# A ring of six row buffers in place of eight under the expert gathers of a hybrid decoder layer

## What is computed

```python
e = i1 * PEER_KEYS + i2
gate = jax.nn.softmax(c_top, axis=-1)
act = jax.nn.gelu(jnp.einsum('thkd,td->thk', u_tab[e], xt).astype(jnp.float32), approximate=False)
w = (gate * act).astype(xt.dtype)
return jnp.einsum('thk,thkd->td', w, v_tab[e])
```

## Time and profile before

| What | us |
|---|---|
| Median of 3 runs (lowest, highest) | 3116.35 (3115.84, 3116.93) |
| Profiled execution, its own time | 3116.56 |
| Its span in the trace | 3114.8 |
| First gather issued, from the span's start | 460.5 |
| Last gather issued | 3085.2 |
| PE, DVE, ACT, POOL busy | 2304.2, 2071.9, 1330.3, 1176.2 |
| Moved by the gathers' queue | 1082.80 MB |

### The profile page before, as it was taken

One profiled execution on the slowest core, in us unless ns is written; L12 is line 12 of the kernel. 1 busy time (PEld: TensorE's weight loads), 2 busy tenths in 40 slices (PEclk: granted clock), 3 DMA queues, 4 the chain that ended last, 5 costly groups with the idle time before them and its releaser, 6 DMA issues.

```text
span 3114.8 us, 35490 instructions
## 1 busy us (share of the span) xinstructions
PE 2304.2 (74%) x11776; PEld 846.1 (27%) x11776; DVE 2071.9 (67%) x4903; ACT 1330.3 (43%) x3979; POOL 1176.2 (38%) x1077
## 2 busy tenths in 40 slices
PE   9998847777777777677676777677767777777775
PEld 5555522222222222232222222222222222222111
DVE  2997426666677777777666666666666666666664
ACT  1023514444355555554544444444444444444433
POOL 1001004444444444454444444444444444433442
PEclk9999979898789888999888888978888788887776
DMA  5002139999999999999999999999999999999997
GB/s 213 21 27 72 59 147 420 421 420 421 420 415 410 421 414 411 417 415 419 408 417 421 421 421 421 420 421 416 418 420 417 421 417 419 416 422 418 418 413 312
DMA packets 165608, 1139.68 MB, mean 366 GB/s; under 512 B 18608, under 2 KB 21040, under 8 KB 32688
## 3 DMA queue, kind: packets, MB, share of 16 engines
q0 software_dynamic: 150096, 1082.80, 84.1%
q1 hardware_dynamic: 15328, 54.62, 4.6%
HBM read 1122.06 MB, written 15.28 MB: 365 GB/s over the span
## 4 chain that ended last, share of the span: by engine, by line
DMA 47%; PE 19%; ACT 10%; DVE 6%; issue 4%; POOL 0%; SPq 0%; DVEq 0%; POOLq 0%; ACTq 0%
DMA ring<-table,e_odd 25%; DMA ring<-table,e_even 20%; PE acc L1623 11%; DVE ring L1426 5%; PE qq_ps L1597 4%; ACT diag L1191 2%; ACT weight L1184 2%; ACT L1258 1%; ACT L1177 1%; ACT gelu L1258 1%; PE proj L1570 1%; ACT wide L1215 1%; PE acc L1661 1%; DVE wide L1441 1%; DMA mix_dram<-mix_t 1%
## 5 line engine op out<-in xcount | busy, mean ns | idle before, releaser
L1623 PE MATMUL acc<-ring,diag 64*64 64x512 f32 x8192 | 1330.7, 735 | 729.0 <-ACT diag L1191 704.8
L1426 DVE CUSTOM_DVE_ANT_0 ring<-ring,xn_odd 128x1024 f32<-128x1024 f32 x512 | 626.7, 1224 | 388.4 <-DMA ring<-table,e_odd 191.0
L1040 POOL DMA_INDIRECT ring<-table,e_even x512 | 578.2, 1129 | 797.8 <-PE acc L1623 698.9
L1426 DVE CUSTOM_DVE_ANT_0 ring<-ring,xn_even 128x1024 f32<-128x1024 f32 x512 | 626.8, 1224 | 364.3 <-DMA ring<-table,e_odd 174.7
L1040 POOL DMA_INDIRECT ring<-table,e_odd x512 | 570.5, 1114 | 724.1 <-PE acc L1623 676.3
L1258 ACT ACTIVATE gelu<-dots 128x1 f32<-128x1 f32 x1024 | 205.9, 201 | 1259.0 <-DVE dots L1426 1246.4
L1623 PEld LDWEIGHTS acc<-ring,diag 64*64 64x64 f32 x8192 | 250.5, 150 | 1511.7 <-ACT diag L1191 1338.9
L1191 ACT ACTIVATE diag<-pairs,weight 128x64 f32<-128x64 f32 x1024 | 356.0, 348 | 33.6
L1597 PE MATMUL qq_ps<-wq_rest,xnT_cur 128*128 128x256 f32 x896 | 262.3, 430 | 0.0
L1597 PEld LDWEIGHTS qq_ps<-wq_rest,xnT_cur 128*128 128x128 f32 x896 | 172.3, 208 | 172.9 <-issue 153.0
L1184 ACT ACTIVATE weight<-gelu,gate_even 128x1 f32<-128x1 f32 x512 | 150.7, 294 | 16.7
(11 more groups left out here) (237 smaller groups left out, 2098.4 us busy)
## 6 DMA issues: line engine op xcount, KB each, us to landing
ring<-table,e_even POOLq DMA_INDIRECT x512
ring<-table,e_odd POOLq DMA_INDIRECT x512
wq_rest<-wq SPq DMA_DIRECT2D x7, 1024.0 KB, 12.8
w_own<-w_units SPq DMA_DIRECT2D x10, 512.0 KB, 3.7
xT<-xt SPq DMA_DIRECT2D x8, 520.0 KB, 7.4
h_next<-x SPq DMA_DIRECT2D x8, 512.0 KB, 19.4
wide<-w_out SPq DMA_DIRECT2D x2, 2048.0 KB, 8.8
wide<-w_out SPq DMA_DIRECT2D x1, 4096.0 KB, 17.4
```

Source lines behind the costliest of these rows:

```text
L1040: pool.indirect_dma_start(out=ring[:, g % RING, :], out_offset=None, in_=table[:, :], in_offset=bass.IndirectOffsetOnAxis(ap=e_row[m % 2][ ...
L1426: dve.tensor_tensor_reduce(ring[:, g % RING, 0:D], ring[:, g % RING, 0:D], xn[(m // PH) % 2][:], 1.0, 0.0, ALU.mult, ALU.add, dots[:, k:k ...
L1623: ins = pe.matmul(acc[ACC_OF[t]][ROWS[j], HALF[i]], diag[ROWS[i], g % DIAGS, :], ring[ROWS[i], g % RING, D + j * 512:D + (j + 1) * 512], s ...
```

## The change

The number of row buffers becomes 6. Nothing else is edited.

```diff
--- before.py
+++ after.py
@@ -35,7 +35,7 @@
 TOPK = 16
 QH = 128
 CAND = TOPK * TOPK
-RING = 8
+RING = 6
 DIAGS = 4
 HP = P // 2
```

## The result

| | us |
|---|---|
| Before, median (lowest, highest) | 3116.64 (3115.84, 3117.58) |
| Changed, median (lowest, highest) | 3164.55 (3161.26, 3174.57) |
| Ratio, 95% interval | 1.0159 (1.0136 to 1.0182) |
| Changed, profiled execution and its span | 3174.57, 3172.8 |

The change costs 48 us. Executions of the changed kernel differ more than those of before (13 us from lowest to highest against 1.7), and the profiled one is the longest of the four. It loses 58 us, where the median loses 48; sums made on its trace are to be read with that in mind.

A forecast was written before the change was run, and what follows sets the result against it. The prediction took DMA to bound the kernel. Dry spells in the frames (26 us), behind the projection weights' load (4.3) and in tiles 4 to 7 (3) gave 33 us on 3116.56, adjusted to 3149; range 3124 to 3186.

The forecast's parts named there:

- The two issues less at the start: At the start, gathers 6 and 7 issue later, but five queued gathers keep the DMA busy until 478.8 us; no cost.
- The plain stream: Outside the attention, some 750 gathers keep 9.8 us in the queue, more than the needed 5.8 or 6.7; no cost.
- The frames, 26 us: In 16 attention frames, the `o` = 15 gather's mean 10.1 us falls 1.6 short of 11.7; 16 x 1.6 = 26 us.
- the load, 4.3: Behind the 4 MB load of the projection's weights, a gather has 7.4 us where 11.7 is needed; 4.3 us lost.
- I count one spell for a frame: In each attention frame, one dry spell is counted, though the two or three gathers behind it are short too.
- I let these two stand against each other: In the frames, engines catching up after a dry spell and late landings pushing DVE, ACT, PE back were taken to offset.
- The 6.7 us that a gather needs: Issue to dot in the last frame with the queue empty, taken as a gather's need; 5.8 kept for the lower end.
- POOL's longest wait in a frame stays at 5 to 6 us: Sign of being right: in the attention frames POOL's longest wait for `b_free` is still 5 to 6 us.
- some 399 GB/s in the attention: Sign of being right: during the attention the DMA rate falls from 415 to about 399 GB/s, 736 us becoming some 765.
- dips behind each `o` = 15 issue: Sign of being right: in the attention frames the DMA rate falls in dips behind each `o` = 15 issue.
- The queue is still deep enough: Rival: a gather needs 4.3 us, so only two frames and the place behind the load lose; 5.6 us, 3122; chance 0.13.
- The engines' chain takes the whole of it: Rival: every frame loses the full 4.98 us, 80 us, plus 7 outside, 3203; chance of whole loss or more 0.13.

The follow-up runs named there:

- look-ahead six outside only: Against the eight-buffer kernel before: look-ahead eight for gathers 142 to 429, six gathers ahead elsewhere; 3119.16 us, ratio 1.0008.
- the ladder: Against the eight-buffer kernel before: look-ahead lowered to 1 through 6 gathers in single steps of tiles 4 to 6, outside the attention; ran once, 3344.89 us.
- the look-ahead of six in the frames: Against the eight-buffer kernel before: look-ahead six only for gathers 142 to 429 (attention frames and behind the weights' load), eight elsewhere; 3161.07 us, ratio 1.0158.
- the early scores: Against the six-buffer change: PE's scores of `o` = 0, 2, 4 put ahead of their place's combine; 3133.33 us, ratio 1.0056 to the kernel before.

## Why the prediction was right, and where it was off

The forecast was 3149, with a range of 3124 to 3186; measured are 3164.55. The sign, the place and the mechanism (dry spells of the DMA in the frames) hold; the size is 48 us in place of 33, and the spells are more than one a frame.

- **The two issues less at the start, no cost.** Right: 420 GB/s up to 794 us.
- **The plain stream, no cost.** Right for six buffers (3 us, not to be told from none, by the kernel with look-ahead six outside only), but on a weak reason. I called it safe because 9.8 us in the queue were left where a gather needs 5.8 to 6.7. That 9.8 is one place, with 4.5 us from landing to issue; the ladder shows 8.35 us at another. At the next step down the rate of such a stretch falls from 420 to 378 GB/s, and five buffers lose some 83 us here. There was hardly any margin.
- **The frames, 26 us, and the load, 4.3.** Right in place, a third too small: 45 us came with the look-ahead of six in the frames and behind the load. Two steps of the working failed. First, "I count one spell for a frame": the last frame has three dips, of 2.1, 1.2 and 4.5 us, and the first, with 12.2 us where I asked for 11.7, has two, about 2 us together, where the working gives none. Second, "I let these two stand against each other": the early scores, which take away DVE's wait for PE, save 31 us of the 48, so what pushes the engines back weighs more than what softens. They may do so by the order of the combines too.
- **The 6.7 us that a gather needs.** As the limit under which the DMA runs short it was too low. A gather alone takes 5.8 us (the ladder; the last frame's `o` = 13 gather too, behind 3 us of standing still), but with seven buffers a limit of 6.7 asks for 9.2 us, which only the tenth frame, the last and the place behind the load lack, by 1.0, 2.5 and 1.8: 5.3 us, where 12.5 were lost. Full rate is seen with 8.8 us from issue to dot. No run gives the limit more closely than between these two.
- **PE's clock, not in the sum.** In the frames PE takes 30 us longer for the same matmuls, at a granted clock of 0.84 in place of 0.88. That is both a result of the waiting and a piece of the hold, and no run takes it apart.
- **POOL's longest wait in a frame stays at 5 to 6 us, some 399 GB/s in the attention, dips behind each `o` = 15 issue.** The wait is 5.85 us in the last frame, as before; the rate is 387 in the profiled execution, the longest of the four. The deep dip lies two places earlier, around the issue of `o` = 13, since the ring is two shorter. I had read the low point off the place where eight buffers have it.
- **The rivals.** "The queue is still deep enough" needed 4.3 us a gather. The data do begin to move some 1.5 us after the issue (1539.78 to 1541.2), as it said, but the rate comes back over four slices, and 3122 fell. "The engines' chain takes the whole of it", 3203, fell in size, but its mechanism is in the result: the real case lies between forecast and this rival. The fixed cost of about 2.0 us that the Trainium skill gives in DMA: Bandwidth & Descriptors, section "Anatomy of one DMA", would have led to the first of them: an estimate of 4.4 us for this gather, where the ladder shows 5.8.

So the range held on the right mechanism, with a middle too small by 15 us. That it wasn't further off is in part luck: the dips that the working didn't have are short, and the limit of 6.7, taken from a row with a slow restart in it, was nearer to the truth than the 5.8 of a gather alone.

## What to carry to other kernels

When a stream is bound by DMA, count for each buffer of its ring the time from landing to the next issue where it is longest, not on the mean and not at one place (here 4.5 us at one, 8.35 at another of the same stream). Add what a transfer needs when the queue is not to run short, which is more than one alone takes (here somewhere from 6.7 to 8.8 us for 1 MB gathers, against 5.8), and compare the sum with the ring's whole round. Losing buffers then costs a little at first and much later: 12, 35, 154 us one after another. Before taking a buffer away, or in place of adding one, look at what holds it: an order on PE that let the scores go ahead of a waiting combine won back 31 of the 48 us with no memory at all, and made seven buffers as good as eight within what can be told.

## What the runs showed of the hardware that was not expected

- The rate of gathers of 128 rows of 8 KB against how many are issued and not yet combined: 106, 213, 298, 346, 378, 420 GB/s for 1 to 6, each from one stretch of one execution. The shortfall at 5 is in separate dips with full rate between them. Behind a dry spell a second dip follows though three more gathers are issued by then (2830.86, 2832.36, 2833.63 us); what in the sixteen DMA engines makes it was not tried.
- Executions of the three kernels with six gathers ahead in the frames and all else as before (the change, and the look-ahead of six everywhere and in the frames) spread over 13, 18 and 20 us (3154 to 3174 with the look-ahead of six in the frames only), those of five buffers over 14, and those of kernels with a full queue over 2 to 6. Why was not tried.
- PE's clock makes the hold behind ACT's stop longer, before the change already. In the last frame of before PE stands 4.76 us for a diagonal. The granted clock, 1.00 (2.4 GHz) from 1482 to 1486 us, is 0.50 (1.2 GHz) when PE goes on, and two combines in a row take 3.34 us:

```profile
1490.13 3.34 PE L1623 MATMUL acc<-ring,diag 64*64 64x512 f32 x16 [4.76 <-ACT diag L1191]
```

```profile
1490.00:1492.40 2.40, 2.27 (x12) 0.75 (x16) 2.40 (x5) 2.21 (x10) 0.00 (x0) 0.50 0.89 372
```

POOL's issue at 1492.41 waits for the first of the two. One combine by itself takes 1.99 us at a granted 0.50 (the ladder's look-ahead 1 stretch) and 1.09 at 1.00 (the plain stream of before):

```profile
1895.60 1.99 PE L1624 MATMUL acc<-ring,diag 64*64 64x512 f32 x8 [7.88 <-ACT diag L1192]
```

```profile
2050.41 1.09 PE L1623 MATMUL acc<-ring,diag 64*64 64x512 f32 x8 [0.72 <-ACT diag L1191]
```

In a frame this is up to 0.9 us of the very hold that empties the queue.
